# Gate and up of the feed-forward blocks by seven block products instead of eight, with the sums of weight blocks on GpSimd and the low parts on VectorE

## The reference

```python
D_MODEL = 1024; SEQ = 512; DEC_BATCH = 8; DEC_SEQ = 4; D_FF = 2816

def rmsnorm(x, g):
    xf = x.astype(jnp.float32)
    y = xf * lax.rsqrt(jnp.mean(xf * xf, axis=-1, keepdims=True) + EPS) * g.astype(jnp.float32)
    return y.astype(x.dtype)

def swiglu(h, w_gate, w_up, w_down):
    return (jax.nn.silu(h @ w_gate) * (h @ w_up)) @ w_down

# trunk, for each of the 2 layers i:
    x = x + 0.5 * rmsnorm(swiglu(rmsnorm(x, ng[0]), p['w_ffn_gate'][i, 0],
                                 p['w_ffn_up'][i, 0], p['w_ffn_down'][i, 0]), ng[1])
    ...  # pooling mixer or gated DeltaNet
    x = x + 0.5 * rmsnorm(swiglu(rmsnorm(x, ng[4]), p['w_ffn_gate'][i, 1],
                                 p['w_ffn_up'][i, 1], p['w_ffn_down'][i, 1]), ng[5])
```

## Time and profile before

| what | value |
|---|---|
| median of 3 runs | 2585.25 us (2583.84 to 2585.4) |
| the profiled execution | 2587.87 us, its span 2586.1 us |
| PE busy | 2445.6 us, 95% |
| DVE busy | 1290.9 us, 50% |
| ACT busy | 872.7 us, 34% |
| POOL busy | 233.9 us, 9%, nearly all of it in the DeltaNet |
| mean granted clock of PE | 0.973 of 2.4 GHz |
| first FFN and pooling mixer | 0 to 524 us |
| second and third FFN | 524 to 937 us, 937 to 1351 us |
| DeltaNet | 1351 to 2148 us |
| fourth FFN and output | 2148 to 2586 us |

### The profile page before, as it was taken

The page is one execution under the profiler, slowest core; times in us unless marked ns, Lnnn a source line. Parts: engine busy times, 40 slices in busy tenths (PEclk is TensorE's granted clock), DMA queues, the critical chain, the costliest instruction groups (busy, mean ns, idle before and its releaser), DMA issues. The chain is left out here.

```text
span 2586.1 us, 46586 instructions
## 1 busy us (share of the span) xinstructions
PE 2445.6 (95%) x18483; PEld 2352.9 (91%) x18483; DVE 1290.9 (50%) x2356; ACT 872.7 (34%) x1540; POOL 233.9 (9%) x198
## 2 busy tenths in 40 slices
PE   7999998699999999999988899999999998999997
PEld 6999998599999989999987798888987988999997
DVE  4443443754344454334435756757566446433444
ACT  4322232333122342212325546363452324322332
POOL 0000000000000000000002122142223640000000
PEclk9999999899999999999998899999999998999999
DMA  3242331022323313422312244424445342232231
GB/s 103 87 124 71 89 97 56 20 73 87 92 81 90 89 58 89 120 82 84 100 46 84 77 112 116 112 67 126 130 117 145 102 137 61 82 103 76 82 99 57
DMA packets 427016, 234.18 MB, mean 91 GB/s; under 512 B 38524, under 2 KB 417045, under 8 KB 426364
## 3 DMA queue, kind: packets, MB, share of 16 engines
q1 hardware_dynamic: 426907, 232.71, 31.3%
HBM read 205.10 MB, written 27.93 MB: 90 GB/s over the span
## 5 line engine op out<-in xcount | busy, mean ns | idle before, releaser
L887 PE MATMUL acc<-hhi,whi 128*128 128x272 f32 x2688 | 775.4, 288 | 2.6 <-DVE wlo L1908 2.6
L887 PE MATMUL acc<-hlo,whi 128*128 128x272 f32 x2688 | 776.0, 289 | 0.0
L887 PE MATMUL acc<-hhi,wlo 128*128 128x272 f32 x2688 | 773.7, 288 | 0.0
L887 PEld LDWEIGHTS acc<-hhi,whi 128*128 128x128 f32 x2688 | 506.0, 188 | 3.8 <-DVE wlo L1908 2.6
L887 PEld LDWEIGHTS acc<-hhi,wlo 128*128 128x128 f32 x2688 | 506.4, 188 | 0.0
L887 PEld LDWEIGHTS acc<-hlo,whi 128*128 128x128 f32 x2688 | 504.9, 188 | 0.0
L1908 DVE TENSOR_TENSOR wlo<-wraw,whi 128x1024 fp32r<-128x1024 f32 (+1 forms) x240 | 319.5, 1332 | 236.2 <-ACT whi L1418 236.1
L887 PE MATMUL acc<-hidhi,whi 128*128 128x272 f32 x1232 | 355.8, 289 | 5.7 <-DVE wlo L1908 5.7
L887 PE MATMUL acc<-hidhi,wlo 128*128 128x272 f32 x1232 | 357.6, 290 | 0.0
L887 PE MATMUL acc<-hidlo,whi 128*128 128x272 f32 x1232 | 355.2, 288 | 0.0
L1418 ACT ACTIVATE whi<-wraw 128x1024 fp32r<-128x1024 f32 (+1 forms) x238 | 269.5, 1133 | 253.7 <-PE acc L887 220.2
(11 more groups left out here) (296 smaller groups left out, 3144.0 us busy)
## 6 DMA issues: line engine op xcount, KB each, us to landing
wraw<-in_w_ffn_gate_dram SPq DMA_DIRECT2D x88, 512.0 KB, 3.8
wraw<-in_w_ffn_up_dram SPq DMA_DIRECT2D x88, 512.0 KB, 3.8
wraw<-in_w_ffn_down_dram SPq DMA_DIRECT2D x64, 704.0 KB, 4.6
wraw<-in_dn_w_in_dram SPq DMA_DIRECT2D x48, 512.0 KB, 4.2
room<-in_state_delta_dram SPq DMA_DIRECT2D x16, 512.0 KB, 4.7
out_delta_sample_dram<-room SPq DMA_DIRECT2D x16, 512.0 KB, 3.5
wraw<-in_dn_w_out_dram SPq DMA_DIRECT2D x16, 512.0 KB, 5.0
room<-x_blocks SPq DMA_DIRECT2D x16, 256.0 KB, 4.0
```

The lines of the kernel that those rows point to most:

```text
L887: last = pe.matmul(acc[s][0:width, hf, 0:HT], w[s][:, k, 0:width], a[:, k0 + k, cols(hf)], start=(n == 0), stop=(n == 3 * nk - 1))
```

## The change

The input of each FFN is normed on DVE (`normed`), and its low and high parts made anew, into the blocks that the new products need: `t_h` and `t_l` hold three combinations of blocks (`difference`, low parts on POOL at L906), `hhi` and `hlo` four (`high_quarter`, `low_quarter`).

The 22 tiles of an FFN are now 11 pairs in four chunks of 2, 3, 3 and 3 pairs. A step is one load of 1 MB: a pair of tiles (256 columns of the weight) of gate or of up, or a pair of output tiles of down. Steps of gate and up in chunk 0 are plain (96 matmuls). In the nine pairs of chunks 1 to 3 a step (`seven`) is the product of a 2x2 of weight blocks by a 2x2 of input blocks in seven products of 12 matmuls, 84 in all. There are 72 such steps. Around the seven products: four sums of weight blocks on POOL (`weight_sums`), a rounding on ACT and a low part on DVE for each of the seven operands (128x512 each), and additions on DVE of the products in all eight banks of PSUM. Operands go through a ring of eight. `by_vector` puts every low part of a seven-product step on DVE; low parts of plain and of down steps are POOL's (L886). Down runs after each chunk, over 4 or 6 tiles, and so adds to `y` four times per output tile and half where it was two. Its number of matmuls is unchanged.

All loops of the FFNs are written out. The 2 MB of zeros are stored from a constant, in 16 pieces during the second FFN, with no wait for POOL.

```diff
+FFN_CHUNKS = ((0, 2), (2, 3), (5, 3), (8, 3))
+RING = 8
+A11, S2, S3, S1, A22, S4, A12 = range(7)
+def by_vector(step, i):
+    return True if step.seven else step is steps_of(step.e)[0]
...
@@ SP
+            def load(step):
+                if step.raw >= 2:
+                    pools, dves = LOW_ENDS[step.raw - 2]
+                    sp.wait_ge(lo_pool, pools)
+                    sp.wait_ge(lo_dve, dves)
...
-                sp.wait_ge(zero_r, 1)
-                for dst in (x_blocks, u_blocks):
-                    sp.dma_start(dst.rearrange("i m j -> i (m j)"), zeros).then_inc(zero_in, 16)
@@ POOL
+            def weight_sums(step):
+                raw = raws[step.raw % 2]
...
+                pool.wait_ge(raw_in[step.raw % 2], 16 * (step.raw // 2 + 1))
+                if at:
+                    pool.wait_ge(*low_ready(sevens[at - 1].op + S4))
+                a11, a21, a12 = raw[:, 0:HK4, 0, :], raw[:, 0:HK4, 1, :], raw[:, HK4:KT, 0, :]
+                pool.tensor_tensor(wsum[:, 0], a21, raw[:, HK4:KT, 1, :], ALU.add).then_inc(s_sum, 1)
+                pool.wait_ge(s_sum, step.sums + 1)
+                pool.tensor_tensor(wsum[:, 1], wsum[:, 0], a11, ALU.subtract).then_inc(s_sum, 1)
+                pool.tensor_tensor(a21, a11, a21, ALU.subtract).then_inc(s_sum, 1)
+                pool.wait_ge(s_sum, step.sums + 2)
+                pool.tensor_tensor(wsum[:, 2], a12, wsum[:, 1], ALU.subtract).then_inc(s_sum, 1)
@@ PE
+            def seven(step, held):
...
+                for i, (h_high, h_low) in enumerate((b11, t2, t3, t1, t4, b22, b21)):
+                    b, o = product_bank(step, i), step.op + i
+                    if b in held:
+                        pe.wait_ge(*held[b])
+                    held[b] = emptied[i]
+                    pe.wait_ge(*low_ready(o))
+                    for k in range(HK4):
+                        for n, (w, h) in enumerate(((w_h, h_high), (w_l, h_high), (w_h, h_low))):
+                            last = pe.matmul(banks[b], w[o % RING][:, k, :], h[:, k, :], start=(k == 0 and n == 0),
+                                             stop=(k == HK4 - 1 and n == 2))
+                    last.then_inc(prod, 1)
@@ ACT
+                    if step.kind == "gate":
+                        round_four(step, nxt)
+                        for i, s in ((4, 3), (5, 2), (6, 1)):
+                            round_op(nxt, i)
+                            silu_seven(step, s)
+                        silu_seven(step, 0)
@@ DVE, in a step of seven products; nxt is the step after it
+                    if nxt.seven:
+                        low_of(nxt, A11)
...
+                    if nxt.seven:
+                        low_of(nxt, S2)
+                    dve.wait_ge(snap, step.sums // 4 + 1)
+                    add(S2, u2, p1, p6)
+                    if nxt.seven:
+                        low_of(nxt, S3)
+                    dve.wait_ge(comb, step.comb + 1)
+                    add(S3, u3, u2, p7)
+                    if nxt.seven:
+                        low_of(nxt, S1)
+                    dve.wait_ge(comb, step.comb + 2)
+                    add(S1, into[:, 3, :], u3, p5)
+                    add(S1, u4, u2, p5)
+                    if nxt.seven:
+                        low_of(nxt, A22)
+                    add(A22, into[:, 2, :], u3, p4)
+                    if step.kind == "up":
+                        dve.wait_ge(gate_silu, step.gates)
+                        times_silu(3, 3)
+                        times_silu(5, 2)
+                    if nxt.seven:
+                        low_of(nxt, S4)
+                    dve.wait_ge(comb, step.comb + 4)
+                    add(S4, into[:, 1, :], u4, p3)
+                    if step.kind == "up":
+                        hidden_low(step, 0, 3)
+                        times_silu(8, 1)
+                        hidden_low(step, 1, 2)
+                    if nxt.seven:
+                        low_of(nxt, A12)
+                    add(A12, into[:, 0, :], p1, p2)
+                    if step.kind == "up":
+                        hidden_low(step, 2, 1)
+                        times_silu(10, 0)
+                        hidden_low(step, 3, 0)
```

More of the change, by code:

```diff
@@ L55, in unit_shape, with plain, seven, tiles @@
 def unit_shape(unit):
[L57 to L61, removed]
+    return KT, (P if unit > IN_BASE else 2 * HV)
+FFN_CHUNKS = ((0, 2), (2, 3), (5, 3), (8, 3))
+RING = 8
+A11, S2, S3, S1, A22, S4, A12 = range(7)
+@dataclass(frozen=True)
+class Step:
+    e: int
+    chunk: int
+    kind: str
+    p: int
+    raw: int
+    op: int
+    ops: int
+    comb: int
+    res: int
+    sums: int
+    gates: int
+    ups: int
+    @property
+    def plain(self):
+        return self.kind != "down" and self.chunk == 0
+    @property
+    def seven(self):
+        return self.kind != "down" and self.chunk > 0
+    @property
+    def tiles(self):
+        return 2 * FFN_CHUNKS[self.chunk][1]
+    @property
+    def halved(self):
+        return self.kind == "down" and self.chunk == 3 and self.p >= 2
+    def m_s(self, i):
+        return divmod(i, 2) if self.plain or self.halved else (i % 2, i // 2)
+    def last_op(self, m):
+        return self.op + (2 * m + 1 if self.plain or self.halved else m + self.ops - 2)
@@ new lines, in round_four, with hidden @@
+                def round_four(step, nxt):
+                    for i in range(2):
+                        round_op(nxt, i)
+                    take_first(step)
+                    for i in range(2, 4):
+                        round_op(nxt, i)
+                def hidden(step, s, count):
+                    m, hf = divmod(s, 2)
+                    tile = 2 * step.p + m
+                    act.wait_ge(comb, step.comb + count)
+                    act.activation(hid[:, tile, 0, cols(hf)], hidf[:, s, :], ACT.Copy).then_inc(hid_hi, 1)
@@ new lines, in ffn @@
+                low_quarter(3)
+                dve.wait_ge(h_lo, H_LO[r] + 20)
+                for step in steps[5:8]:
+                    if step.p == 3:
+                        for i in (A11, S2, S3):
+                            low_of(steps[8], i)
+                    for m in range(2):
+                        for hf in range(2):
+                            evict(step, m, hf)
+                    if step.p == 3:
+                        for i in (S1, A22, S4, A12):
+                            low_of(steps[8], i)
@@ L2021, in ffn @@
+                for step in steps[-4:-2]:
+                    for n in range(4):
+                        evict(step, n // 2, n % 2)
+                        if 4 * step.p + n >= 3:
+                            add_square(r, 4 * step.p + n - 1)
+                    if e == 0 and step is steps[-3]:
                         for b in range(2):
@@ L2066, in _ @@
+                for n in range(8, 12):
+                    mt, hf = TILES_F[n]
+                    evict(steps[-4 + mt // 2], mt % 2, hf)
+                    if n < 11:
+                        add_square(r, n - 1)
             dve.memset(eps[:], EPS)
```

1022 lines of the change are left out of this document (611 added, 411 removed).

## The result

The changed kernel takes 2589.41 us (median of 20 runs) beside 2584.73 for the kernel before on the same chip: ratio 1.002, 95% interval 1.0011 to 1.0028, 4.7 us slower. One of the 20 runs was slow as a whole, 2674.22 us at a granted clock of 0.832, and is left out of the ratio. I forecast 2571 us, faster. The profiled execution has a span of 2590.1 us against 2586.1: +4.0.

What follows compares the result with a forecast made beforehand. PE, busy 95% of the span, was taken as the bound, with DVE deciding whether removed matmuls pay. 2586.1 - 19 + 5 + 24 - 22 - 8 + 2 + 4 = 2572.1 us span, so 2571 us; 8-in-10 range 2515 to 2622.

Steps and rivals of the forecast that it cites:

- GpSimd's sums hold VectorE up, and PE waits for low parts: Chunks 1 to 3: sums block DVE 21.1 us a chunk; a chunk takes 107.1 us, 1.6 less than before; -19 us in all.
- the clock's 0.4 us a chunk: Slow clock after the wait of some 3.6 us before A12, mostly absorbed because DVE sets the pace: +5 us in all.
- chunk 0, 6 us an FFN: Waits of 2.5 us in the second up step and 2 in down, 1.5 for slow clock; four times, +24 us.
- The last pair of down: End of the down loop: PE's 3.97 us wait for instructions and 1.5 of slow clock vanish when written out; -22 us.
- The rival "code": Written-out code doesn't run without a break; the loop-end waits come back elsewhere: +22 us, 2593 us; chance 0.10.
- The zeros' 8 us: Third FFN: PE's 5.73 us wait for weights behind the zeros in SP's queue, and the slow clock after it, go: -8 us.
- the longer first load: Start of the kernel: first load is 1 MB instead of 512 KB, +2 us.
- the past's products in the first FFN: First FFN: transposes of the pool's past stand between down steps and PE waits for DVE's copy: +4 us.
- DVE falls further behind: Up steps in chunks 1 to 3: POOL exceeds its turn or engine waits exceed 0.1 us; slower, 2619 us; chance 0.27.
- DVE keeps up: POOL's phases fall mostly in DVE's idle time and PE waits only 2 us a chunk: 2501 us; chance 0.13.

Runs made afterwards that it cites:

- e5: Changed kernel with 16 useless matmuls (2.0 us) on PE before the wait for A12's low part in a chunk's fifth step: 2575.96 us, ratio 0.9968.
- e1: Changed kernel with GpSimd's weight sums made only in each FFN's first seven-product step, elsewhere only counted: 2490.05 us, ratio 0.9625.
- e4: Changed kernel; in chunk 0 GpSimd makes the fourth plain step's low parts before two low parts of input differences: 2569.13 us, ratio 0.9943.
- e12: Kernel before, with the loop over two pairs of down units in each FFN's second half written out: 2583.48 us, ratio 0.9994.
- e13: Kernel before; the last down pair's first product waits only for the first unit's low part, the second's is awaited behind it: 2560.65 us, ratio 0.9917.
- e2: Changed kernel with only the first and third of four sums made, except in each FFN's first seven-product step: 2487.86 us, ratio 0.9629.
- e3: Changed kernel with the four weight sums of each step made by VectorE, behind low part S4, instead of GpSimd: 2516.57 us, ratio 0.9728.
- e11: Changed kernel; products wait for low parts only before their last four matmuls, plus 16 fill matmuls before the fifth step's A12: 2575.34 us, ratio 0.9964.

## Why the prediction was wrong

The mechanism was right; two terms of the sum were too small, by 10 and 20 us, and together they turn its sign. The rest of the sum erred some 10 us the other way, by luck, which hid a part of it.

- **GpSimd's sums hold VectorE up, and PE waits for low parts: right, and to the size.** I laid out 70.9 us for the six steps without the clock's part. The chunk of the fourth FFN in which the clock stayed up took 70.73 and e5's chunks 70.79. The longest wait is before A12, 3.4 us where I had 3.6. e1 gives it from the other side: without the sums 99 us come back, where 12 x (70.7 - 63.4) = 88 and the clock's part make 103. The rule that I cited from the Trainium skill ("SBUF — State Buffer", "Who interferes with whom") holds in these runs: two-input instructions of DVE last 1.47 to 1.75 us beside a sum and 0.43 and 0.69 alone, and additions with PSUM stay at 0.44.
- **The step that failed first in the sum: the clock's 0.4 us a chunk.** I argued that VectorE would still set the pace when the clock was back. In fact the fifth step's wait is the last long one, and behind it PE waits only 1.0 us more for VectorE. That much of the slow stretch is swallowed at most, the rest is lost: 71.90 - 70.73 = 1.2 us in the chunk shown, where part of the slow stretch lay in the idle time, and 73.22 - 70.73 = 2.5 in each chunk of the third FFN, where it began after product A12, 0.9 us of that last wait was still there, and next to nothing was swallowed. 864.5 us for twelve chunks against 12 x 70.73 = 848.8 is 15.7 us, 1.3 a chunk, where the sum has 5.
- **The step that failed most: chunk 0, 6 us an FFN, measured 11.** I had the place right (the second up step, behind two low parts of differences) but 2.5 us for the wait. The four low parts behind them take POOL 6.0 us, and PE needs the first two: a wait of 4.2 us, and a half clock behind it (a matmul lasts 0.56 at 74.56). e4 takes 6.6 of the 11 us away. Left are 2.7 in down, where I had 2, and 2.0 of smaller waits in the plain steps, which I had not charged. This term alone is 20 us, more than the 18 between forecast and result.
- **The last pair of down: the 22 us are right, their cause wrong.** I read the row "issue" as a wait for code at a loop's end, and charged a rival with its return. e12 and e13 show a wait for the second unit's low part. The changed kernel has a ring of eight blocks rounded ahead and one wait for each block, which I take to be why the wait is gone there, though no run takes this apart. That it is written out is hardly the reason: e12 writes the old kernel's loop out and gains nothing. The rival "code" did not come: PE has no wait called issue in the FFNs of the changed kernel.
- **The rest came out 9 to 11 us better than forecast.** The zeros' 8 us are right: the changed kernel has no wait for weights of 5 us in the third FFN. I charged 2 us for the longer first load; PE's first gate product began at 19.27, against 19.49 before, so nothing. I charged 4 us for the past's products in the first FFN; the break in PE's FFN work is 5.7 us there, but the kernel before has 3.9 for the same products, which I had not looked up. The other 5 to 7 us are small differences in the loops of before and at the ends of the FFNs that I haven't traced.
- **The rivals.** "DVE falls further behind" had the right sign and place but not the mechanism: VectorE kept the times I gave it. "DVE keeps up" is what e1 and e2 are, 2490 us, near the 2501 that I gave it; it was two sums a step away.

## What to carry to other kernels

Work that is moved to GpSimd is not off VectorE if VectorE reads two tiles in SBUF meanwhile: price it as VectorE's time from the trace, and put it on VectorE when it is quicker there (here 0.69 us against about 0.9 to 1.1 of blocking; 73 us between the changed kernel and e3). When one engine's order has slack only up to a threshold, count how far from it the sum is: two sums cost nothing, the fourth cost 4.7 us a chunk. And a wait that the profile calls issue is to be tested against the code's own waits, by what other engine ended just before it, before a cause is named; here that is worth 24 us to the old kernel.

## What I had not expected of the hardware

Sixteen matmuls whose results are thrown away, 2 us of work, made the kernel 13 us faster (e5): an idle time of 3.4 us on PE was followed by a half clock in 11 of 12 chunks, one of 1.3 us, in e5, in none. In the twelfth the same idle time, with the same instructions around it, cost nothing, and in e4 it cost nothing in three, so the price can't be read off one chunk. Nor is a short idle time a safe one: in e11 1.2 us, with 1.4 for ACT behind it, were followed by a half clock in four chunks of 12. And the exclusion works in GpSimd's favour: its sums, with means of 1345 to 1577 ns, are at most 0.3 us over the 1.28 us of the earlier trace rows, while DVE's instructions of 0.43 us take 1.5.
